# Reordering a linear-attention mixing stage: exponent in three parts on VectorE, projections between level products, Fourier rows apart, norm roots ahead of attention

## The reference, cut to what matters

```python
px, pz = split_in(hx), split_in(hz)
a_x = fourier_mix(px['fourier'])                     # 2-D FFT over tokens and 64 channels, real part
b_x = neighborhood_attention(...)                    # NA: 4 heads, window bias from na_rpb, plus context keys
oz_gla, s_f, s_b = bidir_gla(*gla_prepare(pz, *gates), s0, s0)
ox_gla, _, _ = bidir_gla(*gla_prepare(px, *gates), s_f, s_b)
c_x = gla_output(ox_gla, px['gla_r'], gla_norm)      # rms norm over 64, times silu(r)
d_x = block_attention(...)                           # GQA: 4 heads on 2 key heads, with context keys
out_x = jnp.concatenate([a_x, b_x, c_x, d_x], axis=-1)
```

## Time and profile before

| | us |
|---|---|
| median of the runs | 3531.02 |
| profiled execution, its own time | 3530.87 |
| its span, first to last instruction | 3529.0 |
| mean granted TensorE clock | 0.977 of full |
| busy: TensorE (matmuls) | 3388.7, 96% |
| busy: VectorE, ScalarE, GpSimd | 1622.6, 565.6, 45.5 |
| mixing of layer 0, GLA values to output projection | 1977.34 to 2174.65 |
| mixing of layer 1, the same | 3139.02 to 3262.23 |

### The profile page before, as it was taken

The page is one execution under the profiler, slowest core; times in us unless marked ns, Lnnn a source line. Parts: engine busy times, 40 slices in busy tenths (PEclk is TensorE's granted clock), DMA queues, the critical chain, the costliest instruction groups (busy, mean ns, idle before and its releaser), DMA issues.

```text
span 3529.0 us, 41803 instructions
## 1 busy us (share of the span) xinstructions
PE 3388.7 (96%) x16652; PEld 2773.8 (79%) x16652; DVE 1622.6 (46%) x3349; ACT 565.6 (16%) x1191; POOL 45.5 (1%) x48
## 2 busy tenths in 40 slices
PE   8999999999999999999999888999999999998999
PEld 7787888888888888788885444688887888765888
DVE  5567223245683232255553644565556655444100
ACT  2121112111211022100003224100011000133100
POOL 0000000000000000000000010000000000010000
PEclk9999999999999999999999899999999999998999
DMA  5877547636876476333232120232322323222454
GB/s 178 223 198 240 174 147 211 164 117 172 228 219 197 151 207 182 100 90 102 72 91 60 54 48 13 72 101 78 87 81 72 108 72 93 59 90 37 131 161 114
DMA packets 655632, 440.70 MB, mean 125 GB/s; under 512 B 24336, under 2 KB 654512, under 8 KB 655312
## 3 DMA queue, kind: packets, MB, share of 16 engines
q1 hardware_dynamic: 652416, 430.28, 42.4%
q0 software_dynamic: 1552, 6.07, 1.0%
q10 hardware_dynamic: 1472, 1.68, 0.2%
HBM read 436.94 MB, written 1.05 MB: 124 GB/s over the span
## 4 chain that ended last, share of the span: by engine, by line
PE 92%; DVE 4%; ACT 2%; issue 1%; DMA 0%; POOL 0%; ACTq 0%; DVEq 0%
PE psum L1796 46%; PE psum L1988 23%; PE psum L2011 11%; PE psum L2207 2%; PE psum L1933 2%; PE psum L1803 2%; PE psum L2189 1%; DVE arena L1671 0%; PE psum L2152 0%; PE psum L2134 0%; PE psum L1872 0%; PE psum L1812 0%; PE psum L2092 0%; PE psum L2176 0%; PE psum L1858 0%
## 5 line engine op out<-in xcount | busy, mean ns | idle before, releaser
L1796 PE MATMUL psum<-hh,ring 128*128 128x256 f32 (+2 forms) x5344 | 1262.8, 395 | 7.9 <-ACT hh L1160 4.8
L1796 PEld LDWEIGHTS psum<-hh,ring 128*128 128x128 f32 (+1 forms) x5344 | 1010.5, 191 | 236.8 <-issue 102.4
L1796 PE MATMUL psum<-arena,ring 128*128 128x256 f32 x1568 | 343.2, 382 | 8.2 <-DVE arena L1530 5.5
L1796 PEld LDWEIGHTS psum<-arena,ring 128*128 128x128 f32 x1568 | 299.7, 191 | 51.4 <-DVE arena L1530 6.3
L1988 PE MATMUL psum<-hh,arena 128*128 128x256 f32 x1056 | 252.8, 383 | 8.1 <-issue 5.6
L1988 PE MATMUL psum<-hh,ring 128*128 128x256 f32 x1056 | 247.1, 388 | 4.1 <-ACT hh L1160 4.0
L1988 PE MATMUL psum<-arena 128*128 128x256 f32 x1056 | 239.0, 379 | 0.0
L1988 PEld LDWEIGHTS psum<-hh,ring 128*128 128x128 f32 x1056 | 205.2, 195 | 35.4 <-issue 4.7
L1445 DVE SCALAR_TENSOR_TENSOR arena<-arena,par 128x255 f32<-128x255 f32 (+14 forms) x480 | 225.1, 469 | 17.0
L2011 PE MATMUL psum<-arena 128*128 128x256 f32 x1056 | 231.8, 379 | 0.0
L1988 PEld LDWEIGHTS psum<-hh,arena 128*128 128x128 f32 x1056 | 202.3, 192 | 37.0 <-issue 9.2
(11 more groups left out here) (262 smaller groups left out, 2854.3 us busy)
## 6 DMA issues: line engine op xcount, KB each, us to landing
ring<-in_ffn_w SPq DMA_DIRECT2D x176, 512.0 KB, 5.1
ring<-in_w_mod SPq DMA_DIRECT2D x72, 1024.0 KB, 7.6
ring<-in_w_in SPq DMA_DIRECT2D x54, 1024.0 KB, 5.3
ring<-in_w_up SPq DMA_DIRECT2D x88, 512.0 KB, 5.5
ring<-in_w_in SPq DMA_DIRECT2D x84, 512.0 KB, 5.3
ring<-in_w_down SPq DMA_DIRECT2D x16, 1408.0 KB, 7.0
ring<-in_ffn_w SPq DMA_DIRECT2D x12, 1536.0 KB, 6.6
ring<-in_ffn_w SPq DMA_DIRECT2D x12, 1280.0 KB, 5.8
```

The source lines that it names most:

```text
L1796: ins = mm(o[0:rows_, 0:T], w[:, k, c0:c0 + rows_], src[:, k, 0:T], start=(k == 0), stop=(k == kt - 1))
```

## The change

`g_exp` is split into three parts: part 0 the running sums and state slots, part 1 levels 0 to 3, part 2 levels 4 to 7. Each part has its own exponential on ScalarE. A new step `g_mul` does the products of a part, all on VectorE; GpSimd keeps the bias loads alone. The scores wait for part 1, the second level step for part 2. Between level steps stand a projection after the first (`one`) and one after the third (`two`). Fourier rows (`four1`) and columns (`four2`) become separate steps with other work between. `g_n` keeps TensorE's sum and ScalarE's root and moves ahead of attention in both halves; its VectorE work becomes the step `g_d`, within attention at passes 5, 7, 9, 11 (layer 0) and 3, 5 (layer 1). The bias flips move into pass 1. `out` takes its eight products in another order and waits for the last two outputs of attention only before the products that read them. GLA's buffers for x and the context no longer overlap (the raw output of x goes over the decayed-out queries and keys of `glaqk`, that of the context into `raw_z`).

The list, cut to its core:

```diff
-    def gla_scores(s):
+    def gla_level(s, lp):
+        p.step("g_lv", l, s, lp)
+        for hd in range(4):
+            p.job("g_lv", l, s, hd, lp)
+
+    def gla_scores(s, one, two):
         p.step("g_x", l, s)
         for hd in range(4):
             p.job("g_x", l, s, hd)
-        for lp in range(GLA_LEVELS // 2):
-            p.step("g_lv", l, s, lp)
-            for hd in range(4):
-                p.job("g_lv", l, s, hd, lp)
+        gla_level(s, 0)
+        one()
+        gla_level(s, 1)
+        gla_level(s, 2)
+        two()
+        gla_level(s, 3)
...
         if t == 1:
-            p.step("g_exp", l, 1)
+            p.step("g_exp", l, 1, 0)
             if last:
-                p.step("g_exp", l, 0)
+                p.step("g_exp", l, 0, 0)
+        elif t > 1:
+            p.step("g_exp", l, s_first, t - 1)
+            if t == 2:
+                p.step("g_mul", l, 1, 0)
+                if last:
+                    p.step("g_mul", l, 0, 0)
     if last:
-        fourier_in()
-        values(0)
+        fourier_in(0)
+        fourier_in(1)
+        for part in (1, 2):
+            p.step("g_mul", l, 0, part)
+        fourier_rows(0)
+        value(0)
+        gla_keys()
+        fourier_cols(0)
+        p.step("na_load", l)
         gla_state()
-        fourier()
-        gla_scores(0)
-        values(1, 2, 3)
+        gla_scores(0, lambda: value(1), lambda: value(2))
+        value(3)
+        gate_r(0)
+        gate_r(1)
     else:
-        values(0)
+        value(0)
+        for part in (1, 2):
+            p.step("g_mul", l, 1, part)
+        gla_keys()
+        value(1)
         gla_state()
-        gla_scores(1)
-        fourier_in()
-        values(1, 2)
+        gla_scores(1, lambda: fourier_in(0), lambda: fourier_in(1))
+        fourier_rows(0)
+        p.step("g_exp", l, 0, 0)
+        value(2)
+        fourier_cols(0)
+        fourier_rows(1)
         gla_out(1)
-        p.step("g_exp", l, 0)
-        fourier()
-        gla_scores(0)
-        values(3)
-    for i in range(2):
-        p.step("rp", l, i)
-        p.job("rp", l, i, chunk=("w2", l, "glar"))
-    if not last:
+        p.step("g_exp", l, 0, 1)
+        p.step("g_mul", l, 0, 0)
+        p.step("g_exp", l, 0, 2)
+        fourier_cols(1)
+        p.step("na_load", l)
+        for part in (1, 2):
+            p.step("g_mul", l, 0, part)
+        gla_scores(0, lambda: value(3), lambda: gate_r(0))
+        gate_r(1)
         gla_norm(1)
-    for hd in range(4):
-        p.step("na_bias", l, hd)
-        p.job("flip", l, hd)
     gla_out(0)
+    gla_norm(0)
     units = mix_units(last)
+    scale_at = {3: (0, 0), 5: (0, 1)} if last else {5: (1, 0), 7: (1, 1), 9: (0, 0), 11: (0, 1)}
     for n in range(len(units) + 4):
         if n < len(units):
             p.step("at", l, n)
             for b in range(2):
                 p.job("at", l, n, b)
-        if n == len(units):
-            gla_norm(0)
+        if n == 1:
+            for hd in range(4):
+                p.step("na_bias", l, hd)
+                p.job("flip", l, hd)
+        if n in scale_at:
+            p.step("g_d", l, *scale_at[n])
```

The products (VectorE), the waits (TensorE) and the output projection:

```diff
+                elif kind == "g_mul":
+                    s, part = r
+                    dve.wait_ge(decays, exp_count(l, s, part))
...
+                    if part == 0:
+                        do(tt(e, e, (k if s else q).to_broadcast([P, 2, S]), ALU.mult), decayed, mul_count(l, s, part))
                     else:
...
+                        do(tt(e[:, 0], e[:, 0], q.to_broadcast([P, 4, S]), ALU.mult))
+                        do(tt(e[:, 1], e[:, 1], k.to_broadcast([P, 4, S]), ALU.mult), decayed, mul_count(l, s, part))
...
-                    pe.wait_ge(q_decayed, exp_index(l, s) + 1)
-                    pe.wait_ge(k_decayed, kdec(l, s))
+                    pe.wait_ge(decayed, mul_count(l, s, 1))
...
                     s, lp = r
+                    if lp == 1:
+                        pe.wait_ge(decayed, mul_count(l, s, 2))
...
-                    for k in range(KT):
+                    order = (0, 1, 4, 5, 6, 7, 2, 3)
+                    for k in order:
+                        if i == 0 and k == 4:
+                            pe.wait_ge(gla_ready, gla_count(l, True))
+                        if i == 0 and k in (2, 3):
+                            evacuated(pe, job[("at_o", l, n // 2 - (2 if k == 2 else 1))])
                         src = mixf if k < 2 else mixt
```

More of the change, by code:

```diff
@@ L410, in plan_second, with value, fourier_in, gate_r @@
             p.job("nrot", l, n - 2)
[L412 to L417, removed]
-        for i in range(2):
[L419 to L432, removed]
+    def value(t):
+        p.step("vp", l, t)
+        p.job("vp", l, t, chunk=("w2", l, "v"))
+    def fourier_in(i):
+        p.step("fp", l, i)
+        p.job("fp", l, i, chunk=("w2", l, "four"))
+    def gate_r(i):
+        p.step("rp", l, i)
+        p.job("rp", l, i, chunk=("w2", l, "glar"))
+    def fourier_rows(s2):
+        for t in range(TT):
+            p.step("four1", l, s2, t)
+            p.job("four1", l, s2, t)
+    def fourier_cols(s2):
+        for g in range(2):
+            p.step("four2", l, s2, g)
+            p.job("four2", l, s2, g)
+    def gla_keys():
         p.step("g_kt", l)
         p.job("g_kt", l)
+    def gla_state():
         for d in range(2):
@@ L456, in gla_norm @@
             p.job("g_n", l, s, pr)
+    s_first = 0 if last else 1
     for t in range(2 * TT):
@@ L1275, in _ @@
                     act.wait_ge(n_normed, 7 * l + 7)
-                    if s == 0 and l < DEPTH - 1:
-                        act.wait_ge(gla_ready, gla_index(l, 1, pr) + 1)
                     produced(act, j)
@@ L1681, in _ @@
                 elif kind == "g_exp":
-                    s = r[0]
-                    n = exp_index(l, s)
+                    s, part = r
+                    n = exp_count(l, s, part)
                     one = ones[:, 0:1].to_broadcast([P, S])
-                    if s == 0 and l < DEPTH - 1:
-                        produced(dve, job[("g_lv", l, 1, 3, GLA_LEVELS // 2 - 1)])
-                    do(nc.vector.tensor_tensor_scan(cum_f, one, la[:, 0, s * S:(s + 1) * S], 0.0, ALU.mult, ALU.add))
-                    do(nc.vector.memset(cum_b[:, 0:1], 0.0))
-                    do(nc.vector.tensor_tensor_scan(cum_b[:, 1:S + 1], one, la[:, 1, s * S:(s + 1) * S], 0.0, ALU.mult, ALU.add))
-                    ex = cum_b[:, 0:S]
-                    if not (s == 1 and l == DEPTH - 1):
-                        for lv in range(GLA_LEVELS):
+                    ex = cum_b[:, 0:S]
+                    if part == 0:
+                        do(nc.vector.tensor_tensor_scan(cum_f, one, la[:, 0, s * S:(s + 1) * S], 0.0, ALU.mult, ALU.add))
+                        do(nc.vector.memset(cum_b[:, 0:1], 0.0))
+                        do(nc.vector.tensor_tensor_scan(cum_b[:, 1:S + 1], one, la[:, 1, s * S:(s + 1) * S], 0.0, ALU.mult, ALU.add))
+                        if s == 0:
+                            do(nc.vector.tensor_copy(expo[:, 16, :], cum_f))
+                            do(tt(expo[:, 17, :], cum_b[:, S:S + 1].to_broadcast([P, S]), ex, ALU.subtract), exponents, n)
+                        else:
+                            do(tt(expo[:, 18, :], cum_f[:, S - 1:S].to_broadcast([P, S]), cum_f, ALU.subtract))
+                            do(nc.vector.tensor_copy(expo[:, 19, :], ex), exponents, n)
+                    else:
+                        if s == 0 and l < DEPTH - 1:
+                            produced(dve, job[("g_lv", l, 1, 3, GLA_LEVELS // 2 - 1)])
+                        for lv in range(4 * part - 4, 4 * part):
                             m = P >> lv
```

99 lines of the change are left out of this document (33 added, 66 removed).

## The result

| | before | after |
|---|---|---|
| median of four runs on one chip, us | 3531.07 | 3490.74 |
| range, us | 3530.93 to 3534.79 | 3488.80 to 3492.71 |
| profiled execution, span, us | 3529.0 | 3490.1 |
| mean granted clock | 0.977 | 0.984 |
| GpSimd busy, us | 45.5 | 23.6 |

The ratio is 0.9882, with a 95% interval of 0.9870 to 0.9894: 1.2% faster. The forecast was 3485 in a range of 3472 to 3504.

A forecast was written before the change was run, and what follows sets the result against it. TensorE bounds the kernel, with matmuls in 3388.7 of 3529.0 us, so only its queue counts. Terms -35.9 - 8.8 + 3.1 + 13.0 - 20.9 + 3.5 sum to -46.0, giving 3485 us, range 3472 to 3504.

The forecast's parts named there:

- Layer 0's first part: Layer 0 up to attention: 97.9 us against 133.81, 35.9 less, as waits and half-clock work go.
- GpSimd's products: Products moved from GpSimd to VectorE, up to attention: 2.45 us per part, or 4.1 by the mean of two rows.
- step (d) on DMA: Bias table's issues move earlier on GpSimd's queue, ring loads and gate weights are in time: nothing, either way.
- Layer 1's first part: Layer 1 up to attention: 70.8 us against 79.59, 8.8 less, with a new wait of 3.2.
- step (e): Clock: new holes of 3.2 us, and 2.7 to 3.0 at layer 0's products, add 3.5, between 0 and 12.
- Start of attention: Attention's start in both layers: bias additions delay the first softmax on VectorE, 0.85 and 2.3 us later, sum +3.1.
- End of attention: Last-but-one output to first projection, each layer: 13.1 us becomes 3.65; with faster first projections -20.9 in all.
- Products inside: GLA's six products inside attention on VectorE: 8.9 us in layer 0, 4.1 in layer 1, together +13.0.
- Attention pays in full: Rival: attention's products cost 16.6 us and half clock in their holes 8.5, so 3497; chance 0.18.
- All absorbed: Rival: products inside at their low ends, attention's start at -3, no clock loss, so 3472; chance 0.08.
- the split does not do what it says: Rival: scores still wait for the whole exponent, holes of some 8 and 10 us remain, 3503; chance 0.08.
- The slower rival: Rival: 1.2 GHz stays from layer 0's scores on; 3533 for layer 0's attention alone, up to 3700; chance 0.04.

The follow-up runs named there:

- undivided run: Changed kernel with key transposes and scores waiting for the last part's product, as if the exponent were one; ratio 0.9907 to the kernel before.
- the one with levels together: Changed kernel with the two projections behind the four level steps and not between them; ratio 0.9929 to the kernel before.
- the run without the wait: Changed kernel with layer 1's value tile ahead of the Fourier rows and layer 0's part 1 exponential ahead of GLA's output copies; ratio 0.9865 to the kernel before.
- the filler run: Changed kernel with six extra constant products on TensorE ahead of the transposes that wait for each GLA product; 3491.35 us, ratio 0.9873 to the kernel before.
- the run with empty products: Changed kernel with GLA's products inside attention working on 1 column of 256, same order and waits; ratio 0.9835 to the kernel before.

## Why the prediction was right, and where it was off

- **Layer 0's first part** (35.9 less): 36.0. The walk held within about 1 us at the stations that the trace shows: transposes at 1996.05 (1996.5 forecast), the context's scores at 2003.46 (2004.3), the end of the last Fourier columns at 2041.5 (2042.5), the new wait 1.90 (1.5). Matmuls took 94.67 us for 95.0 forecast and the waits 3.1 for 2.8. That the two differences cancel to 0.1 us is luck; the mechanism is not. The undivided run and the one with levels together take its two reasons apart: 9.6 us hang on the split, 15.3 on projections between levels. The rest is some 11 us, if these two may simply be added, which no run tests. 3.6 of it is no gain: the bias flips only moved into attention. Some 8.0 can be read from the Fourier columns: their waits of 4.43 and 0.79 us are gone, and the first pair took 3.62 us for 6.37. No run takes the Fourier split alone, so that share is argued and not shown.
- **GpSimd's products** (2.45 us a part on VectorE): the price was right, 2.5 us (two products of 1.23, the second part starting 2.52 after the first). What taking them off GpSimd gains by itself, the prediction didn't ask. With the bias loads behind them they would cost at most 1.9 and 2.7 us in the two layers. What step (d) on DMA called "nothing, either way" was true only because GpSimd's queue held nothing else; with the products on it the same loads cost 10.
- **Layer 1's first part** (8.8 less): 7.0 less. The wait of 3.2 was 3.08, and 1.6 us of half clock stood behind it (68.88 us of matmuls, and 67.31 in the run without the wait), which the walk left to step (e). A value tile put ahead of it would have cost nothing.
- **Start of attention** (+0.85 and +2.3): from the first unit to the first transposes it took 7.78 us in both layers, for 6.40 and 4.92 before: +1.4 and +2.9. Half a microsecond short in each.
- **End of attention** (13.1 to 3.65): 13.1 to 4.06 in both layers, 0.4 short in each. In these 4.06 the last head's output waits 1.16 us for ScalarE's copy; the prediction doesn't say what it took for that wait. The projection's later waits are worth 0.74 a layer.
- **Products inside** (+8.9 and +4.1): 8.8 and 4.2, once the half clock of the filler run is taken off. This walk was right, as far as one reading tells (layer 1's attention scatters by 1.7).
- **The clock, step (e), was too small.** The prediction named the places (holes of 2.7 to 3.0 us at each product in layer 0, 3.2 in layer 1) and added 3.5 us in all, without working it out. The holes came at three of the four products and in layer 1; the half clock behind them was 4.05 us by the filler run and 1.6 in layer 1's first part, 5.65 together.
- **The sum.** By the profiled executions 38.9 us were gained for 46.0 forecast. Of the 7.1 missing, 2.1 are the clock (5.65 for 3.5), 1.1 the two starts and 0.8 the two ends of attention, 0.3 other differences in the four stretches, and 2.7 lie outside them. There the prediction had 2.0 less, for the first projections at full clock, and the spans say 0.7 more. In layer 0 that projection did come at full clock (1.98 us for 3.78); in the feed-forward behind it a product of eight instructions took 3.65 us for 1.96 before. But what is outside the four stretches moves by more than 2.7 us from execution to execution, so this part has no cause that the runs show. The medians differ by 40.3, 5.7 short of the forecast.
- **Rivals.** "Attention pays in full" (3497) is about as near to the measured 3490.7 as the forecast of 3485. It had half of the truth: the products did not cost their full 16.6 us but 13.0 without the clock, and the clock in the holes did come, at half of its 8.5. "All absorbed" fell with the 12.8 us that the run with empty products gave back, "the split does not do what it says" with the transposes that wait for nothing. The slower rival fell: no stretch stayed at half clock. The rule of the Trainium skill on transposes (TensorE: Matmul & The Clock Gate, section "🔬 Part 4: PE-mode transpose"), weighed in the prediction, finds no support in this kernel: 56 us of attention, with transposes in every pass among other products, ran at a granted clock of 1.00 in the run with empty products. Transposes by themselves were not tried.

## What to carry to other kernels

Put independent matmul work between steps whose results another engine must carry away, which was worth 15.3 and 7.0 us here. Write down for each queue what a moved step is now ahead of: GpSimd's loads ahead of its products cost 10. Work that must share an engine with a pipeline goes in as small pieces where that engine has slack, or whole where it is idle; in layer 0 four whole lumps of 2.8 us cost 12.8, and the same work placed so cost 2.5. Price a hole on TensorE with the slow work behind it, and ask of every insertion whether one long hole wouldn't be cheaper than several short ones: in layer 0's attention one of 8.8 us was, by about 2 us.

## What the runs showed of the hardware

- Extra matmuls in a wait made the stretch shorter: 69.17 us at a granted clock of 0.90 became 65.12 at 1.00 with 48 matmul instructions more. Behind holes of 2.85, 3.29 and 3.02 us in attention the granted clock was 0.50, the lower level of 1.2 GHz (2098 to 2100, 2108 to 2110, 2116 to 2120). A wait of 2.2 us in layer 1 was followed by products at half clock in one kernel (3.58 us for 16 instructions) and at full clock in another (1.95) with the same code there.
- GpSimd's products and VectorE's subtractions hold each other up, both ways: a 1024-column product that GpSimd started amid VectorE's subtractions took 3.91 us, while the subtractions kept their 0.28; two with nothing beside them took 4.09 together; and a subtraction that started 0.07 us after a GpSimd product took 2.09 for 0.28.
- The same instructions ahead of the mixing ended 8 us apart from execution to execution on some chips (1976.8 to 1985.2 us). What decides it wasn't tried.
